# A three-layer model on one core: x's high parts written by ScalarE, low parts taken by VectorE from the turned tiles, and a square that runs one unit behind its product

## The chip, the cores and the metric

The kernel runs on one core of a Trainium2 chip. The metric is the device time of one execution in microseconds (us). Five engines work side by side: TensorE (PE, whose weight loads are shown apart as PEld), VectorE (DVE), ScalarE (ACT), GpSimd (POOL) and SyncE (SP), which here issues the loads of the weights. They meet only at semaphores, and each engine runs its own instructions in the order written.

## What is computed

The input x has 256 tokens of width 1024. Three layers follow: retention, forgetting attention, and a block that has two mixers side by side (dilated window attention and HGRN2) and then a feed-forward part. Cut to what the change touches:

```python
x = x + gate[:, None, :] * y                      # end of the second layer (forgetting attention)
x = _rms_norm(x, final_g)                         # h, the input of the third layer
u = rmsnorm(h, norm1_w[l]); proj = u @ w_in[l]    # "mixers": 7 chunks of 512 columns
ya = dilated_attention_group(qa, ka, va)
yb = hgrn2_group(qb, fb, ib, gb, lb_table[l], hgrn_norm_w[l])
h = h + jnp.concatenate([ya, yb], axis=-1) @ w_out[l]
u2 = rmsnorm(h, norm2_w[l]); gu = u2 @ w_gate_up[l]
h = h + (silu(gate) * up) @ w_down[l]             # "feed-forward"
```

## The kernel before

Every product of float32 matrices is made of three matmuls in a rounded format (fp32r): each operand is split into a high part (its rounded value) and a low part (the rest), and the product is high by high (L354), high by low (L355) and low by high (L356). The operands from x are `ahi` and `alo`, 128x256 for each block of 128 columns, the weights are `whi` and `wlo`.

The weights come as a stream of units of 512 KB, which is two blocks of 128 rows by 512 columns. For each unit SP loads `raw` (8 buffers), ACT writes `whi` (3 buffers; before it writes unit v it waits until PE has finished unit v-3), DVE subtracts to get `wlo`, and PE runs `unit`: 12 matmuls of 512 columns, 6 for each half m of the tokens. On ACT and DVE the call `ring_to(u + 2)` makes the parts of the unit that is two ahead of the one PE is at. All other work of these two engines is written by hand between these calls, so what stands in front of a `ring_to` delays the weights behind it.

Where a layer begins, x has to stand with its columns on the partitions. PE turns four 128x128 blocks of x into one PSUM bank (`x_turn`, 12 of them, n = 0 to 11; n = 4 to 7 belong to the mixers and 8 to 11 to the feed-forward). Before, all twelve then go one way: ACT scales the four blocks from PSUM into a float32 stage in SBUF (`x_act`), DVE copies the stage into `ahi`, rounded, in two instructions, and subtracts to get `alo` in two more (`x_split`). PE may use a block when its `alo` is there (`x_ready`). The four T banks of PSUM go round: `bank()` gives the next one, and PE waits there until the reader of the bank's last tile is done.

The norm in front of the mixers is a double one (of x, and of x times the gain `fg`). So during the first units of the mixers, for each of the four quarters k of x, DVE forms the product `f2` = x * `fg` (signal `f_prod`, L1027 "arena<-x,arena"), and ACT squares and sums first x (`square`, L1765 "acc<-x") and then `f2` (L1765 "acc<-arena", signal `sf1`). `norm_f` on DVE needs all eight sums; ACT takes two roots for it.

Later in the mixers the HGRN2 heads end with `hg_values` (L951, L953, L954), two tiles of PSUM that are made right after the last `values` of the window attention.

Of the kernel before, what the change touches and what calls it, by code (L numbers as in the profile page):

```python
# [6 lines left out]
P = 128  # L7
# [158 lines left out]
def program(nc, x_in, c_in, pos_in, mod_w, mod_b, norm_g, ret_w_in, ret_w_out, fox_w_in, fox_b_f,  # L166
            fox_q_gain, fox_k_gain, fox_w_out, final_g, norm1_w, w_in2, lb_logits, hgrn_nw, w_out2,
            norm2_w, w_gate_up, w_down, final_nw, consts, out):
    with ExitStack() as ctx:
# [154 lines left out]
        def _(e):  # L324
# [7 lines left out]
            def bank(name, sem, n, i=None):  # L332

                if i is None:
                    i = at[0] % 4
                    at[0] += 1
                if ring[i] is not None:
                    on_.wait_ge(*ring[i])
                ring[i] = (sem, n)
                bank_of[name] = i  # L340
                return T[i]
# [50 lines left out]
            def x_turn(src, k0, m):  # L392

                n = turns[0]
                turns[0] += 1
                t = bank(("x", n), sig["x_act"], 2 * SPLIT_ORDER.index(n) + 2)
                transposes(t, [src[:, m, k * P:(k + 1) * P] for k in range(k0, k0 + 4)], "x_turned")

            def x_ready(slot, k0, m, n):
                p = SPLIT_ORDER.index(n)  # L400
                for z in range(2):
                    for k in range(2):
                        ready[slot + k0 + 2 * z + k, m] = (sig["x_split"], 4 * p + 3 + z)


            def turn_x0(k):
# [536 lines left out]
            on_.wait_ge(sig["near"], 16)  # L943
            on_.wait_ge(sig["far"], 1)
            for m in range(2):
                t = bank(("hg_values", m), sig["hg_norm"], 4 + m)
                for h in range(4):
                    vv = vb[:, :, h * P:(h + 1) * P]
                    o = t[:, h * P:(h + 1) * P]
                    if m == 0:  # L950
                        d = e.matmul(o, SH[:, 0, h, :], vv[:, 0, :], start=True, stop=True)  # L951
                    else:
                        e.matmul(o, SH[:, 1, h, :], vv[:, 0, :], start=True, stop=False)  # L953
                        d = e.matmul(o, SH[:, 2, h, :], vv[:, 1, :], start=False, stop=True)  # L954
                d.then_inc(sig["hg_values"], 1)
# [64 lines left out]
        def _(e):  # L1020
# [5 lines left out]
            def tt(o, a, b, op, name):  # L1026
                e.tensor_tensor(o, a, b, op).then_inc(sig[name], 1)  # L1027
# [118 lines left out]
            def x_split(n, slot, k0, m, stage):  # L1146

                p = SPLIT_ORDER.index(n)
                ms = slice(m * P, m * P + P)
                for z in range(2):  # L1150
                    on_.wait_ge(sig["x_act"], 2 * p + z + 1)
                    copy(ahi[:, slot + k0 + 2 * z:slot + k0 + 2 * z + 2, ms], stage[:, (2 * p + z) % 4, :, :], "x_split")
                for z in range(2):
                    b = slot + k0 + 2 * z
                    on_.wait_ge(sig["x_split"], 4 * p + 1 + z)
                    tt(alo[:, b:b + 2, ms], stage[:, (2 * p + z) % 4, :, :], ahi[:, b:b + 2, ms].bitcast(F32), ALU.subtract, "x_split")

            stage1 = acc[:, 2048:3072].rearrange("p (z n s) -> p z n s", z=4, n=2)

# [307 lines left out]
                elif n < 3:  # L1467
                    left_low(10 + 2 * n)
            u_out = {0: u + 1, 1: u + 3}
            stage2 = gate[:, 0, :].rearrange("p (z n s) -> p z n s", z=4, n=2)  # L1470
            ring_to(u + 2)
            ring_to(u + 3)
            add_gated(0, 0, 0, 1, 1, sgf, -1)
            add_gated(1, 0, 1, 1, 1, sgf, -1)
            ring_to(u + 4)
            x_split(4, 16, 0, 0, stage2)
            x_split(5, 16, 0, 1, stage2)
            ring_to(u + 5)
            add_gated(2, 1, 0, 1, 1, sgf, 0)
            add_gated(3, 1, 1, 1, 1, sgf, 1)  # L1480
# [102 lines left out]
            for k in range(4):  # L1583
                ring_to(u + 2)
                u += 1
                if k == 0:
                    x_split(6, 16, 4, 0, stage2)
                    x_split(7, 16, 4, 1, stage2)
                c, m = k // 2, k % 2
                cs_ = slice(512 * c, 512 * c + 512)  # L1590
                on_.wait_ge(sig["mix_in"], 32)
                on_.wait_ge(sig["res1"], 2 * k + 2)
                tt(f2[:, m, cs_], x[:, m, cs_], fg[:, cs_], ALU.mult, "f_prod")
# [94 lines left out]
            add_plain(0, 0, 2)  # L1688
            add_plain(0, 1, 2)
            ring_to(u + 4)  # L1690
            x_split(8, 22, 0, 0, stage2)
            x_split(9, 22, 0, 1, stage2)
            ring_to(u + 5)
            add_plain(1, 0, 2)
            add_plain(1, 1, 2)
# [16 lines left out]
            for c in range(6):  # L1712
                for k in range(4):
                    ring_to(u + 2)
                    u += 1
                    if c == 0 and k == 0:
                        x_split(10, 22, 4, 0, stage2)
                        x_split(11, 22, 4, 1, stage2)
                    if c == 0 and k == 2:
                        r = st[:, 72:74]  # L1720
                        sx = st[:, 64:68].rearrange("p (m c) -> p m c", c=2)
                        on_.wait_ge(sig["sq2"], 4)
                        tt(r, sx[:, :, 0], sx[:, :, 1], ALU.add, "rms2")
                        on_.wait_ge(sig["rms2"], 1)
                        root(r, r, D, "rms2", 0, "rms2_act", 1)
                    if c > 0 and k < 2:
                        left_low(4 * (c - 1) + 2 * k)
                if c < 5:
                    for k in range(4):
                        ring_to(u + 2)  # L1730
# [29 lines left out]
        def _(e):  # L1760
# [31 lines left out]
            def x_act(n, stage, k0, f, scale, shift=None):  # L1792

                p = SPLIT_ORDER.index(n)
                t = T[bank_of["x", n]]
                on_.wait_ge(sig["x_turned"], n + 1)
                for z in range(2):
                    on_.wait_ge(sig["x_split"], 4 * (p - 2) + 3 + z)
                    for i in range(2):
                        k = 2 * z + i  # L1800
                        act(stage[:, (2 * p + z) % 4, i, :], t[:, k * P:(k + 1) * P], f, "x_act" if i else None,
                            scale=scale(k0 + k), bias=shift(k0 + k) if shift else 0.0)

            def sqrt_table():
                on_.wait_ge(sig["filled"], 2)
# [273 lines left out]
                if n in (1, 2):  # L2079
                    left_high(10 + 2 * n)  # L2080
            sqrt_table()
            stage2 = gate[:, 0, :].rearrange("p (z n s) -> p z n s", z=4, n=2)
            ring_to(u + 4)
            on_.wait_ge(sig["rows_read"], 3)
            x_act(4, stage2, 0, ACT.Copy, lambda k: col(n1f, k))
            x_act(5, stage2, 0, ACT.Copy, lambda k: col(n1f, k))
            ring_to(u + 5)
            u += 4

# [18 lines left out]
            def turned_win(n):  # L2108
                m = n % 2
                from_four("wqk", n, (qA, kA)[n // 2][:, :, m * P:(m + 1) * P], ACT.Copy, (0.125, 1.0)[n // 2])  # L2110

            ring_to(u + 2)
            u += 1
            x_act(6, stage2, 4, ACT.Copy, lambda k: col(n1f, k))
            x_act(7, stage2, 4, ACT.Copy, lambda k: col(n1f, k))
            on_.wait_ge(sig["left_turned"], 12)
            for k in range(4):
                if k:
                    ring_to(u + 2)
                    u += 1  # L2120
                c, m = k // 2, k % 2
                cs_ = slice(512 * c, 512 * c + 512)
                square(c, m, 1, 2 * k + 2)
                on_.wait_ge(sig["f_prod"], k + 1)
                on_.wait_ge(sig["sq1"], k + 1)
                act(xn1[:, m, cs_], f2[:, m, cs_], ACT.Square, "sf1", accum=st[:, 68 + 2 * m + c:69 + 2 * m + c])
            for k in range(4):
                ring_to(u + 2)
                u += 1
# [78 lines left out]
                    left_high_scaled(2 * n, 2 * n - 4)  # L2208
            sqrt_table()
            ring_to(u + 4)  # L2210
            x_act(8, stage2, 0, ACT.Copy, lambda k: col(n2_col, k))
            x_act(9, stage2, 0, ACT.Copy, lambda k: col(n2_col, k))
            ring_to(u + 5)
            u += 4

# [4 lines left out]
            for c in range(6):  # L2220
                for k in range(4):
                    ring_to(u + 2)
                    u += 1
                    if c == 0 and k == 0:
                        x_act(10, stage2, 4, ACT.Copy, lambda k: col(n2_col, k))
                        x_act(11, stage2, 4, ACT.Copy, lambda k: col(n2_col, k))
                        on_.wait_ge(sig["left_turned"], 16)
                    if c == 0 and k < 2:
                        for m in range(2):
                            square(k, m, 2, 2 * k + m + 1)  # L2230
                    if c == 0 and k == 2:
                        on_.wait_ge(sig["rms2"], 2)
                        act(st[:, 72:74], st[:, 72:74], ACT.Sqrt, "rms2_act")
                    if c > 0 and k < 2:
                        left_high(4 * (c - 1) + 2 * k)
# [141 lines left out]
```

## Time and profile before

| | |
|---|---|
| median of 3 runs | 735.34 us (732.81 to 736.9) |
| the profiled execution | 736.37 us, span of its core 734.6 us |
| PE busy | 709.7 us, 97% of the span |
| DVE busy | 502.1 us, 68% |
| ACT busy | 380.3 us, 52% |
| mean granted TensorE clock | 0.986 (0.78 in the first 20 us, 1.00 from 60 us to 720 us) |

The span goes from the first to the last instruction; the other 1.8 us of that execution lie around it. The first layer fills the time to about 235 us, the second ends at about 393 us, the mixers begin at about 397 us, the feed-forward at about 541 us. PE is busy nearly all the time, so the stretches where it waits are what matters, and most of the idle time of ACT and DVE costs nothing.

### The profile page before, as it was taken

What the parts mean: (1) busy time and instruction counts of PE and PEld (TensorE: products, weight loads), DVE (VectorE), ACT (ScalarE), POOL (GpSimd) and SP (SyncE); (2) the same over time, 40 slices, a digit from 0 to 9 for tenths busy, and PEclk for the clock granted to TensorE, in tenths of its full rate; (3) what the DMA queues carried; (4) which work ended last, traced back from release to release, by engine and by line L of the source; (5) the groups of instructions that cost most, each with busy time, mean ns of one, the idle gap of its engine ahead of it and who ended that gap; (6) DMA issues with size and microseconds to landing.
All of it is one profiled execution on the core that took longest, in us unless ns stands there. A gap on an engine that the chain in (4) does not pass through costs nothing.

```text
span 734.6 us, 9409 instructions
## 1 busy us (share of the span) xinstructions
PE 709.7 (97%) x3556; PEld 580.8 (79%) x3556; DVE 502.1 (68%) x727; ACT 380.3 (52%) x559; POOL 15.9 (2%) x33
## 2 busy tenths in 40 slices
PE   6999999999999899999999899999999999999996
PEld 5887877777887778878887688887888888888884
DVE  4699887787945868755668599965675555655444
ACT  5347544565534646564555654554565454444343
POOL 6000000000000000000000000000000000000000
PEclk8799999999999999999999999999999999999999
DMA  9999855676964357842454453333456556555611
GB/s 294 370 354 308 298 194 182 201 224 214 309 242 130 123 195 256 266 134 89 138 173 148 141 175 109 122 114 116 139 176 210 189 175 189 182 196 176 198 61 57
DMA packets 74476, 138.96 MB, mean 189 GB/s; under 512 B 5748, under 2 KB 18272, under 8 KB 74432
## 3 DMA queue, kind: packets, MB, share of 16 engines
q1 hardware_dynamic: 72816, 134.82, 56.6%
q10 hardware_dynamic: 736, 1.90, 0.7%
q0 software_dynamic: 880, 1.64, 0.6%
q8 instruction: 28, 0.46, 0.3%
q14 instruction: 16, 0.13, 0.1%
HBM read 137.31 MB, written 1.05 MB: 188 GB/s over the span
## 4 chain that ended last, share of the span: by engine, by line
PE 87%; DVE 7%; ACT 2%; issue 2%; DMA 1%; SPq 0%; DVEq 0%; ACTq 0%
PE G L354 22%; PE G L356 22%; PE G L355 22%; PE T L375 5%; DVE wlo L1027 2%; PE T L741 2%; PE T L854 2%; DVE arena L1027 2%; PE T L731 1%; PE G L465 1%; DMA arena<-in_mod_w_dram 1%; PE G L467 1%; PE G L466 1%; ACT whi L1767 1%; PE T L416 1%
## 5 line engine op out<-in xcount | busy, mean ns | idle before, releaser
L1027 DVE TENSOR_TENSOR wlo<-raw,whi 128x1024 fp32r<-128x1024 f32 x206 | 251.0, 1223 | 133.6 <-ACT whi L1767 133.0
L354 PE MATMUL G<-whi,ahi 128*128 128x512 f32 x776 | 314.4, 405 | 7.4 <-DVE wlo L1027 6.8
L356 PE MATMUL G<-whi,alo 128*128 128x512 f32 x776 | 303.3, 391 | 0.0
L355 PE MATMUL G<-wlo,ahi 128*128 128x512 f32 x776 | 302.3, 390 | 0.0
L1767 ACT ACTIVATE whi<-raw 128x1024 fp32r<-128x1024 f32 x206 | 217.3, 1061 | 131.9 <-PE G L356 117.3
L354 PEld LDWEIGHTS G<-whi,ahi 128*128 128x128 f32 x776 | 145.9, 188 | 41.4 <-DVE wlo L1027 12.1
L356 PEld LDWEIGHTS G<-whi,alo 128*128 128x128 f32 x776 | 145.6, 188 | 32.2
L355 PEld LDWEIGHTS G<-wlo,ahi 128*128 128x128 f32 x776 | 146.1, 188 | 28.5 <-issue 1.2
L1769 ACT ACTIVATE arena<-T,st 128x128 f32<-128x128 f32 (+2 forms) x56 | 21.7, 478 | 30.5 <-DVE st L1400 30.5
L375 PE MATMUL T<-head,arena 128*128 128x128 f32 x244 | 37.2, 277 | 0.0
L375 PEld LDWEIGHTS T<-head,arena 128*128 128x128 f32 x244 | 29.7, 141 | 9.4 <-issue 2.0
L1767 ACT ACTIVATE ahi<-T 128x512 fp32r<-128x512 f32 x25 | 15.0, 599 | 41.5 <-PE T L375 41.5
L1769 ACT ACT_TABLE_LOAD x27 | 34.6, 1283 | 2.8 <-issue 1.8
L1036 DVE SCALAR_TENSOR_TENSOR acc<-raw,cact,acc 128x1024 f32<-128x1024 f32 x24 | 30.8, 1282 | 1.1
L1027 DVE TENSOR_TENSOR alo<-T,ahi 128x512 fp32r<-128x512 f32 x25 | 17.3, 691 | 17.8 <-ACT ahi L1767 17.7
L1027 DVE TENSOR_TENSOR arena<-arena 128x512 f32<-128x512 f32 (+7 forms) x46 | 23.0, 549 | 0.8 <-ACT arena L1769 0.5
L1400 DVE TENSOR_REDUCE st<-T 128x2 f32<-128x512 f32 (+1 forms) x18 | 11.6, 686 | 15.5 <-PE T L731 15.5
L1769 ACT ACTIVATE st<-st 128x1 f32<-128x1 f32 (+3 forms) x21 | 4.3, 206 | 30.0 <-DVE st L1031 18.3
L1036 DVE SCALAR_TENSOR_TENSOR arena<-arena,cact 128x512 f32<-128x512 f32 (+1 forms) x24 | 16.4, 684 | 0.8
L854 PEld LDWEIGHTS T<-arena 128*128 128x128 f32 x128 | 15.4, 191 | 0.9 <-DVE arena L1027 0.4
L1767 ACT ACTIVATE arena<-arena 128x512 f32<-128x512 f32 x14 | 8.3, 640 | 14.4 <-DVE arena L1027 14.4
L854 PE MATMUL T<-arena 128*128 128x128 f32 x128 | 15.7, 276 | 0.0
(219 smaller groups left out, 576.1 us busy)
## 6 DMA issues: line engine op xcount, KB each, us to landing
raw<-in_ret_w_in_dram SPq DMA_DIRECT2D x48, 512.0 KB, 5.4
raw<-in_w_gate_up_dram SPq DMA_DIRECT2D x40, 512.0 KB, 3.8
raw<-in_mod_w_dram SPq DMA_DIRECT2D x32, 512.0 KB, 5.0
raw<-in_fox_w_in_dram SPq DMA_DIRECT2D x32, 512.0 KB, 4.7
raw<-in_w_in_dram SPq DMA_DIRECT2D x28, 512.0 KB, 3.5
raw<-in_w_down_dram SPq DMA_DIRECT2D x22, 512.0 KB, 4.4
arena<-in_mod_w_dram SPq DMA_DIRECT2D x16, 512.0 KB, 8.3
raw<-in_ret_w_out_dram SPq DMA_DIRECT2D x16, 512.0 KB, 5.5
```

Source lines behind the costliest of these rows:

```text
L354: e.matmul(o, ah, wh, start=first and k == 0, stop=False)
L355: e.matmul(o, ah, wl, start=False, stop=False)
L356: done = e.matmul(o, al, wh, start=False, stop=last and k == 1)
L375: d = e.transpose(t[:, n * P:(n + 1) * P], s, idf)
L416: e.matmul(sums_of(SUMMED[g][i], a), mod_tile(g)[:, a, r, i * P:(i + 1) * P], cact[:, r:r + 1], start=r == r0, stop=False)
L741: d = e.matmul(t[:, 65 * a:65 * a + 65], PT[:, g % 2, (a * (m + 1) + j) * P:(a * (m + 1) + j + 1) * P], v[:, j, h, :], start=j == 0, stop= ...
L854: d = e.matmul(t[:, h * P:(h + 1) * P], k[:, h, m * P:(m + 1) * P], q[:, h, m * P:(m + 1) * P], start=True, stop=True)
L1027: e.tensor_tensor(o, a, b, op).then_inc(sig[name], 1)
L1036: e.scalar_tensor_tensor(out=o, in0=a, scalar=s, in1=b, op0=op0, op1=op1).then_inc(sig[name], 1)
L1400: e.tensor_reduce(st[:, 44 + 4 * r:44 + 4 * r + n], t[:, :].rearrange("p (h n) -> p h n", h=n), AX.X, ALU.max, negate=True).then_inc(sig[f ...
L1767: d = e.activation(o, a, f, scale=scale)
L1769: d = e.activation(o, a, f, scale=scale, bias=bias)
```

## The change

For the turned tiles of the mixers and the feed-forward (n = 4 to 11), ACT writes the scaled blocks straight into `ahi`, rounded (`x_high`), and DVE forms `alo` from the PSUM bank, as scale times the turned block minus `ahi` (`x_low`), in one instruction for each block. The bank of such a tile is now free after DVE's last instruction and no longer after ACT's, and DVE waits until ACT has written all four blocks. The square of `f2` for quarter k runs after the weights and the square of x of quarter k+1 (`square_f`). The two tiles of `hg_values` go to the T banks 1 and 2 and no longer take the next two of the round.

```diff
-                t = bank(("x", n), sig["x_act"], 2 * SPLIT_ORDER.index(n) + 2)
+                p = SPLIT_ORDER.index(n)
+                t = bank(("x", n), *((sig["x_act"], 2 * p + 2) if n < 4 else (sig["x_split"], 4 * p + 4)))
...
-                t = bank(("hg_values", m), sig["hg_norm"], 4 + m)
+                t = bank(("hg_values", m), sig["hg_norm"], 4 + m, 1 + m)
...
+            def x_low(n, slot, k0, m, scale):
+
+                p = SPLIT_ORDER.index(n)
+                t, ms = T[bank_of["x", n]], slice(m * P, m * P + P)
+                on_.wait_ge(sig["x_act"], 2 * p + 2)
+                for k in range(4):
+                    b = slot + k0 + k
+                    stt(alo[:, b, ms], t[:, k * P:(k + 1) * P], scale(k0 + k), ahi[:, b, ms].bitcast(F32), ALU.mult, ALU.subtract, "x_split")
...
-            x_split(4, 16, 0, 0, stage2)
-            x_split(5, 16, 0, 1, stage2)
+            x_low(4, 16, 0, 0, lambda k: col(n1f, k))
+            x_low(5, 16, 0, 1, lambda k: col(n1f, k))
...
+            def x_high(n, slot, k0, m, scale):
+
+                p = SPLIT_ORDER.index(n)
+                t, ms = T[bank_of["x", n]], slice(m * P, m * P + P)
+                on_.wait_ge(sig["x_turned"], n + 1)
+                for k in range(4):
+                    act(ahi[:, slot + k0 + k, ms], t[:, k * P:(k + 1) * P], ACT.Copy, "x_act" if k % 2 else None, scale=scale(k0 + k))
...
+            def square_f(k):
+
+                c, m = k // 2, k % 2
+                cs_ = slice(512 * c, 512 * c + 512)
+                on_.wait_ge(sig["f_prod"], k + 1)
+                on_.wait_ge(sig["sq1"], k + 1)
+                act(xn1[:, m, cs_], f2[:, m, cs_], ACT.Square, "sf1", accum=st[:, 68 + 2 * m + c:69 + 2 * m + c])
...
                 square(c, m, 1, 2 * k + 2)
-                on_.wait_ge(sig["f_prod"], k + 1)
-                on_.wait_ge(sig["sq1"], k + 1)
-                act(xn1[:, m, cs_], f2[:, m, cs_], ACT.Square, "sf1", accum=st[:, 68 + 2 * m + c:69 + 2 * m + c])
+                if k:
+                    square_f(k - 1)
+            square_f(3)
```

ACT's instructions behind the second pair of turned tiles of the mixers, before the change (`acc,st<-x` is the square of x, `acc,st<-arena` that of `f2`; after the last row come the two roots of `norm_f`):

```order
L1765 ACTIVATE acc,st<-x 128x512
L1765 ACTIVATE acc,st<-arena 128x512
L1767 ACTIVATE whi<-raw 128x1024
L1765 ACTIVATE acc,st<-x 128x512
L1765 ACTIVATE acc,st<-arena 128x512
L1767 ACTIVATE whi<-raw 128x1024
L1765 ACTIVATE acc,st<-x 128x512
L1765 ACTIVATE acc,st<-arena 128x512
L1767 ACTIVATE whi<-raw 128x1024
L1765 ACTIVATE acc,st<-x 128x512
L1765 ACTIVATE acc,st<-arena 128x512
L1767 ACTIVATE whi<-raw 128x1024
```

And in the changed kernel, at the same place:

```order
L1773 ACTIVATE acc,st<-x 128x512
L1775 ACTIVATE whi<-raw 128x1024
L1773 ACTIVATE acc,st<-x 128x512
L1773 ACTIVATE acc,st<-arena 128x512
L1775 ACTIVATE whi<-raw 128x1024
L1773 ACTIVATE acc,st<-x 128x512
L1773 ACTIVATE acc,st<-arena 128x512
L1775 ACTIVATE whi<-raw 128x1024
L1773 ACTIVATE acc,st<-x 128x512
L1773 ACTIVATE acc,st<-arena 128x512 x2
L1775 ACTIVATE whi<-raw 128x1024
```

The weights' high part now stands between the square of x and the square of the product that belong together, and two squares of `f2` follow each other at the end.

DVE's instructions at the end of the second layer, where the first two turned tiles of the mixers are split, before the change:

```order
L1027 TENSOR_TENSOR x<-x,acc 128x512
L1027 TENSOR_TENSOR wlo<-raw,whi 128x1024
L1039 CAST ahi<-gate 128x2x128 x2
L1027 TENSOR_TENSOR alo<-gate,ahi 128x2x128 x2
L1039 CAST ahi<-gate 128x2x128 x2
L1027 TENSOR_TENSOR alo<-gate,ahi 128x2x128 x2
L1027 TENSOR_TENSOR wlo<-raw,whi 128x1024
L1027 TENSOR_TENSOR acc<-G2,gate 128x512
```

And in the changed kernel:

```order
L1027 TENSOR_TENSOR x<-x,acc 128x512
L1027 TENSOR_TENSOR wlo<-raw,whi 128x1024
L1036 SCALAR_TENSOR_TENSOR alo<-T2,n1f,ahi 128x128 x4
L1036 SCALAR_TENSOR_TENSOR alo<-T3,n1f,ahi 128x128 x4
L1027 TENSOR_TENSOR wlo<-raw,whi 128x1024
L1027 TENSOR_TENSOR acc<-G2,gate 128x512
```

Eight instructions stand where eight stood; they are half as wide as before, have three inputs, and one of these is in PSUM.

PE's instructions at the last `values` of the window attention (L741) and `hg_values` (L951 and on), before the change (T0 to T3 are the four banks):

```order
L354 MATMUL G1<-whi,ahi 128x512
L355 MATMUL G1<-wlo,ahi 128x512
L356 MATMUL G1<-whi,alo 128x512
L741 MATMUL T3<-arena,gate 128x65 x4
L951 MATMUL T3<-arena 128x128 x4
L953 MATMUL T0<-arena 128x128
L954 MATMUL T0<-arena 128x128
```

And in the changed kernel:

```order
L354 MATMUL G1<-whi,ahi 128x512
L355 MATMUL G1<-wlo,ahi 128x512
L356 MATMUL G1<-whi,alo 128x512
L741 MATMUL T3<-arena,gate 128x65 x4
L951 MATMUL T1<-arena 128x128 x4
L953 MATMUL T2<-arena 128x128
L954 MATMUL T2<-arena 128x128
```

The instructions and their order stay; only the banks move, from 3 and 0 to 1 and 2. The instruction in front of them writes to bank 3.

## Rows read from the trace of the kernel before

**Rows 1.** The page, busy time (share of the span) and instructions of each engine.
```profile
PE 709.7 (97%) x3556; PEld 580.8 (79%) x3556; DVE 502.1 (68%) x727; ACT 380.3 (52%) x559; POOL 15.9 (2%) x33
```
**Rows 2.** PE's waits over the span: us in total, times, longest us.
```profile
PE G L354 <- DVE wlo L1027: 6.8, 10, 1.3
...
PE T L951 <- DVE acc L1027: 0.7, 1, 0.7
```
**Rows 3.** Waits of PE's weight loads, 400 to 424 us.
```profile
PEld G L354 <- DVE wlo L1027: 4.7, 5, 1.2
PEld T L375 <- DVE x L1027: 1.3, 2, 0.9
```
**Rows 4.** Stretches: us, busy of PE, PEld, DVE, ACT, POOL, clock, DMA share, GB/s.
```profile
400.00:424.00 24.00, 20.70 (x89) 15.08 (x88) 15.71 (x31) 15.02 (x34) 0.00 (x0) 1.00 0.46 134
430.00:510.00 80.00, 80.00 (x479) 67.70 (x480) 64.14 (x100) 38.66 (x60) 0.00 (x0) 1.00 0.40 125
535.00:555.00 20.00, 20.00 (x97) 16.50 (x96) 14.29 (x29) 13.89 (x32) 0.00 (x0) 1.00 0.59 189
```
**Rows 5.** PE in order of time: start us, us, instruction, [idle before <-releaser].
```profile
402.71 0.40 PE L356 MATMUL G<-whi,alo 128*128 128x512 f32 x1
...
407.50 0.39 PE L356 MATMUL G<-whi,alo 128*128 128x512 f32 x1
408.68 0.50 PE L354 MATMUL G<-whi,ahi 128*128 128x512 f32 x1 [0.79 <-DVE wlo L1027]
...
425.33 0.39 PE L356 MATMUL G<-whi,alo 128*128 128x512 f32 x1
425.56 1.04 PE L375 MATMUL T<-head,arena 128*128 128x128 f32 x8
...
429.31 1.31 PE L375 MATMUL T<-head,arena 128*128 128x128 f32 x8
```
**Rows 6.** ACT in order of time, same place.
```profile
403.46 0.65 ACT L1765 ACTIVATE acc<-x 128x512 f32<-128x512 f32 x1
...
406.25 1.05 ACT L1767 ACTIVATE whi<-raw 128x1024 fp32r<-128x1024 f32 x1
407.21 0.61 ACT L1765 ACTIVATE acc<-x 128x512 f32<-128x512 f32 x1
...
409.26 0.63 ACT L1765 ACTIVATE acc<-arena 128x512 f32<-128x512 f32 x1 [1.35 <-DVE arena L1027]
...
409.89 1.05 ACT L1767 ACTIVATE whi<-raw 128x1024 fp32r<-128x1024 f32 x1
...
419.86 0.47 ACT L1769 ACTIVATE st<-st 128x2 f32<-128x2 f32 x2 [1.64 <-DVE st L1033]
```
**Rows 7.** DVE in order of time, same place.
```profile
404.90 0.69 DVE L1027 TENSOR_TENSOR arena<-x,arena 128x512 f32<-128x512 f32 x1
407.40 1.23 DVE L1027 TENSOR_TENSOR wlo<-raw,whi 128x1024 fp32r<-128x1024 f32 x1 [1.82 <-ACT whi L1767]
408.55 0.68 DVE L1027 TENSOR_TENSOR arena<-x,arena 128x512 f32<-128x512 f32 x1
```
**Rows 8.** ACT and DVE in order of time, turned tiles.
```profile
394.59 2.18 ACT L1767 ACTIVATE gate<-T,n1f 128x128 f32<-128x128 f32 x8 [2.04 <-PE T L375]
...
395.77 0.29 DVE L1039 CAST ahi<-gate 128x256 fp32r<-128x256 f32 x1 [0.22 <-ACT gate L1767]
...
397.05 0.76 DVE L1027 TENSOR_TENSOR alo<-gate,ahi 128x256 fp32r<-128x256 f32 x2
...
397.82 1.23 DVE L1027 TENSOR_TENSOR wlo<-raw,whi 128x1024 fp32r<-128x1024 f32 x1
...
527.38 0.88 DVE L1661 SCALAR_TENSOR_TENSOR alo<-T,cols,ahi 128x256 fp32r<-128x256 f32 x2 [0.99 <-ACT ahi L1767]
```
**Rows 9.** PE's weight loads and PE in order of time, `hg_values`.
```profile
514.34 0.97 PEld L951 LDWEIGHTS T<-arena 128*128 128x128 f32 x8 [0.79 <-issue]
514.37 1.13 PE L951 MATMUL T<-arena 128*128 128x128 f32 x8 [0.68 <-DVE acc L1027]
```

More of the change, by code:

```diff
@@ L400, in x_ready @@
                 p = SPLIT_ORDER.index(n)
-                for z in range(2):
-                    for k in range(2):
-                        ready[slot + k0 + 2 * z + k, m] = (sig["x_split"], 4 * p + 3 + z)
+                for k in range(4):
+                    ready[slot + k0 + k, m] = (sig["x_split"], 4 * p + (3 + k // 2 if n < 4 else 1 + k))
             def turn_x0(k):
@@ L1469, in _ @@
             u_out = {0: u + 1, 1: u + 3}
-            stage2 = gate[:, 0, :].rearrange("p (z n s) -> p z n s", z=4, n=2)
             ring_to(u + 2)
@@ L1586, in _ @@
                 if k == 0:
-                    x_split(6, 16, 4, 0, stage2)
-                    x_split(7, 16, 4, 1, stage2)
+                    x_low(6, 16, 4, 0, lambda k: col(n1f, k))
+                    x_low(7, 16, 4, 1, lambda k: col(n1f, k))
                 c, m = k // 2, k % 2
@@ L1690, in _ @@
             ring_to(u + 4)
-            x_split(8, 22, 0, 0, stage2)
-            x_split(9, 22, 0, 1, stage2)
+            x_low(8, 22, 0, 0, lambda k: col(n2_col, k))
+            x_low(9, 22, 0, 1, lambda k: col(n2_col, k))
             ring_to(u + 5)
@@ L1716, in _ @@
                     if c == 0 and k == 0:
-                        x_split(10, 22, 4, 0, stage2)
-                        x_split(11, 22, 4, 1, stage2)
+                        x_low(10, 22, 4, 0, lambda k: col(n2_col, k))
+                        x_low(11, 22, 4, 1, lambda k: col(n2_col, k))
                     if c == 0 and k == 2:
@@ L1802, in x_act @@
                             scale=scale(k0 + k), bias=shift(k0 + k) if shift else 0.0)
+            def x_high(n, slot, k0, m, scale):
+                p = SPLIT_ORDER.index(n)
+                t, ms = T[bank_of["x", n]], slice(m * P, m * P + P)
+                on_.wait_ge(sig["x_turned"], n + 1)
+                for k in range(4):
+                    act(ahi[:, slot + k0 + k, ms], t[:, k * P:(k + 1) * P], ACT.Copy, "x_act" if k % 2 else None, scale=scale(k0 + k))
             def sqrt_table():
@@ L2081, in _ @@
             sqrt_table()
-            stage2 = gate[:, 0, :].rearrange("p (z n s) -> p z n s", z=4, n=2)
             ring_to(u + 4)
             on_.wait_ge(sig["rows_read"], 3)
-            x_act(4, stage2, 0, ACT.Copy, lambda k: col(n1f, k))
-            x_act(5, stage2, 0, ACT.Copy, lambda k: col(n1f, k))
+            x_high(4, 16, 0, 0, lambda k: col(n1f, k))
+            x_high(5, 16, 0, 1, lambda k: col(n1f, k))
             ring_to(u + 5)
@@ L2110, in turned_win @@
                 from_four("wqk", n, (qA, kA)[n // 2][:, :, m * P:(m + 1) * P], ACT.Copy, (0.125, 1.0)[n // 2])
+            def square_f(k):
[4 more added lines that the diff above has]
+                act(xn1[:, m, cs_], f2[:, m, cs_], ACT.Square, "sf1", accum=st[:, 68 + 2 * m + c:69 + 2 * m + c])
             ring_to(u + 2)
             u += 1
-            x_act(6, stage2, 4, ACT.Copy, lambda k: col(n1f, k))
-            x_act(7, stage2, 4, ACT.Copy, lambda k: col(n1f, k))
+            x_high(6, 16, 4, 0, lambda k: col(n1f, k))
+            x_high(7, 16, 4, 1, lambda k: col(n1f, k))
             on_.wait_ge(sig["left_turned"], 12)
@@ L2210, in _ @@
             ring_to(u + 4)
-            x_act(8, stage2, 0, ACT.Copy, lambda k: col(n2_col, k))
-            x_act(9, stage2, 0, ACT.Copy, lambda k: col(n2_col, k))
+            x_high(8, 22, 0, 0, lambda k: col(n2_col, k))
+            x_high(9, 22, 0, 1, lambda k: col(n2_col, k))
             ring_to(u + 5)
@@ L2224, in _ @@
                     if c == 0 and k == 0:
-                        x_act(10, stage2, 4, ACT.Copy, lambda k: col(n2_col, k))
-                        x_act(11, stage2, 4, ACT.Copy, lambda k: col(n2_col, k))
+                        x_high(10, 22, 4, 0, lambda k: col(n2_col, k))
+                        x_high(11, 22, 4, 1, lambda k: col(n2_col, k))
                         on_.wait_ge(sig["left_turned"], 16)
```

## The prediction

> **What bounds the kernel now.** The page first: PE is busy 97% of the span, DVE 68%, ACT 52% [rows 1]. So a shorter ACT or DVE instruction is worth nothing by itself; the time moves only where PE waits. The list of PE's waits is short, and it is the second view to read: ten waits for the weights' low part, 6.8 us together, and among the single ones 0.7 us of L951 behind an evacuation by DVE [rows 2]. The third view asks where they are. Between 400 and 424 us PE's weight loads waited five times for `wlo`, 4.7 us, and twice for x, 1.3 us [rows 3], and PE was busy 20.70 of 24 us there, against 80.00 of 80 us from 430 to 510 us [rows 4]. That is the place where the square is moved.
>
> How the waits arise is seen in PE's own order [rows 5]. Matmuls start every 0.228 us when nothing holds them: from 402.71 to 407.50 us are 21 steps, 4.79 us. A unit of 12 is then 2.73 us. But the five units behind 407.50 us, up to the matmul of 425.33, take 17.83 us, or 3.57 us each. ACT shows the period, from one `whi` at 406.25 to the next at 409.89 us, 3.64 us [rows 6], and this is a ring over two engines: `whi` to `wlo` 1.15 us (406.25 to 407.40), `wlo` to the product 1.15 us (to 408.55), product to its square 0.71 us (to 409.26), square to the next `whi` 0.63 us (to 409.89) [rows 6, 7]. ACT stands 1.35 us in front of the square of `f2`, waiting for a product that DVE can only make behind the `wlo` that ACT itself has just released. The ring takes 3.64 us where PE needs 2.73, so PE starves.
>
> **The change part by part.**
>
> *The late square.* With the square of `f2` one unit behind, the product it needs has long been made, and nothing goes round. ACT then has for each unit `whi` 0.96 us (406.25 to 407.21) and two squares of some 0.6 us each (0.63 us from 409.26 to 409.89, which includes reading the sum), together 2.2 us; DVE has 1.15 and 0.7 us, together 1.85 us. Both are below PE's 2.73. To see whether the first stall goes too, I walk through it. The square of x is at 403.5 us as now [rows 6]; the `whi` behind it no longer waits for the product and its square, so it starts at some 404.2 instead of 406.25 us, since its buffer has been free since the end of the unit in front of the second turns. Its `wlo` can start at 405.6 us, behind the product that runs at 404.9 us [rows 7], and ends at 406.8 us; PE asks for it at 407.73 us (407.50 plus a step). So the first stall goes with 0.9 us to spare. The next three `whi` then start at 406.4, 408.6 and 412.2 us (the last behind two squares of `f2`, for whose second it waits until 411.6 us), and their `wlo` end at 408.7, 410.9 and 414.5 us, where PE asks at 410.5, 413.2 and 415.9 us. Behind them comes the wait for `norm_f`'s roots, which ACT waits for 1.64 us now [rows 6]: by the same steps the roots run at 415.0 us, the next `whi` at 415.4 us, its `wlo` ends at 417.7 us and PE asks at 418.7 us. This is the tightest place, 1.0 us of slack.
>
> What the five stalls cost: the five units between the matmul of 407.50 and that of 425.33 us [rows 5] are 60 steps, 13.65 us at 0.2275 each; they took 17.83. Term: **-4.2 us**.
>
> *The turn behind it.* DVE comes late to the second turn after this stretch as well: its eight transposes take 1.31 us where the first eight take 1.04 [rows 5]. The norm's two 128x1024 products that stand in front of it on DVE run when the weights' parts ahead of them are done; with those earlier against PE, most of this goes. Of the 0.27 us I take **-0.2 us**. Bounds 0 and -0.3.
>
> *The banks of `hg_values`.* PE waits 0.68 us at L951 because its tile goes to bank 3, which holds the `values` tile made just before it and still to be read by DVE [rows 9]. Bank 1 held the logits and bank 2 the transposed weights of the attention; both were read before that last `values` could start. The wait goes, and with it the whole chain behind (`hg_values` to ACT's square to the norm) is as much earlier. The weight loads show 0.79 us idle. Term: **-0.7 us**. Seven tiles behind it land in other banks, each long free.
>
> *The low parts.* ACT issues 8 blocks of 128x128 for two tiles before and after, in 2.18 us [rows 8]; that the target is `ahi` and rounded, I cost at nothing, because its writes of this format have no longer rows. DVE had 8 instructions and has 8. No 128x128 instruction with scalar and PSUM input is in the trace. The nearest is the 128x256 one: two take 0.88 us [rows 8], so with 0.48 for the last one step is 0.40 us. 128 columns fewer, at about 1.05 ns per column, leave 0.27 us. From above the bound is that same 0.40 us, from below 0.24 us, where ACT's own pace of 0.27 becomes the limit. Now to the chain. DVE can start when ACT has written four blocks, at 395.77 us, where the second CAST starts now; four steps end at 396.84 us, where the second tile has just become ready (ACT ends at 396.77); four more end at 397.91 us. The next `wlo` starts at 397.82 us now [rows 8]. So it is **+0.1 us** late, and at 0.40 us per step it would be +1.2 us late. This is on the path: behind it stand four instructions that add the layer's output to x, and PE waits for them in front of the second turns (the 1.3 us of [rows 3]). That wait stays. Much below nothing it can't go: at 0.24 us a step the second tile still waits for ACT until 396.8 us and ends at 397.8. At the feed-forward the same eight steps stand, but PE is busy 20.00 of 20 us there [rows 4], so +0.1 is covered and of +1.2 us about 1.0 would be felt. For the second pair of tiles at each place PE comes to the blocks a unit later, so there is cover of more than 1 us.
>
> The Trainium skill, "VectorE: DVE Perf Modes", section "The TRN2 errata", speaks against this part: each instruction pays a fixed latency, about twice as long from PSUM as from SBUF, so many small tiles are dear and tiles should have 512 elements or more. An estimate from its figures (58 cycles fixed from SBUF, 120 from PSUM, at 0.96 GHz, the rounding copy at two columns a cycle) is 2.1 us for the old eight and 2.1 us for the new, so that by the page this term is 0 and the sum -5.1 us. The sum below goes by the rows.
>
> *Sum.* -4.2 - 0.2 - 0.7 + 0.1 = -5.0 us, on the profiled execution of 736.37 us (its span of 734.6 and 1.8 around it): 731.4. The median shown, 735.34, is 1.0 us below that execution; the same sum from it gives 730.3, and I take 730.4.
>
> **The rivals.**
>
> *The stall moves instead of going.* For it speaks the 1.0 us of slack at `norm_f`, worked out with steps that I rounded, and the wait of two squares in a row. Against it: later units have 3 us of slack each, so one late `whi` is caught up. One or two stalls of 0.95 us stay: 731.4 to 732.4.
>
> *What is gained is lost later.* PE comes 4 to 5 us earlier to stages with their own chains (the levels of HGRN2, the window attention). For it: DVE is busy 64.14 of 80 us there. Against it: that stage shows no PE wait of its own at all [rows 4], and its chains start from PE's results, so they move along; the weights' transfers are at a share of 0.40 to 0.46. If half is lost: 733.
>
> *The steps of the low parts cost 0.40 us or more.* At 0.40: 1.1 + 1.0 us of the gain are lost, 732.5. This is also the one that **ends on the other side**: two places, each 8 steps, so 16 times the excess over 0.27 us less the cover of about 0.3 us must be over 5.1 us; from 0.61 us per step on the kernel is slower than before. That is nearly what four times the width takes, 0.68 us [rows 7]. It could come if DVE's reads of PSUM held each other up with ACT's beside them, which no row of before shows. At 0.75 us: 737.7. Against it stands the step of 0.40 us at twice the width [rows 8].
>
> *The change doesn't do what it says.* The squares wait for something else, say because DVE makes the product late again behind a late `wlo`. Then only the bank's 0.7 us is left: 734.6.
>
> **How the numbers follow.** 0.5% (3.7 us) is about what a measurement of this kernel can tell from no change, which puts the line at 731.7 us. Chances: all terms as summed 0.68 (its own range 729 to 731.9), stall moves 0.12, half lost later 0.09, dear steps short of slower 0.05, no effect of the square 0.03, slower 0.03. Of the first case nine tenths are below the line, of the second a half, of the dear steps a third: faster 0.69, and slower by 0.5% 0.02, the rest 0.29. The range goes from 728.4 (the stalls' 4.7 us of idle loads instead of 4.2, and runs as low as 2.5 us under their median are shown, of which a median keeps part) to 733.4, which takes in the moved stall and the dear steps.
>
> **What would show it.** In the profile after: no wait of PE for `wlo` between the second turns and the first chunk's end; ACT's squares of `f2` without idle time in front but for the last; units 2.73 us apart there; L951 without a wait; the 128x128 steps of DVE 0.27 us apart; the wait for x in front of the second turns still there, 0.1 us longer. Wrong it would be made by a wait for `wlo` that stays at the unit behind `norm_f`'s roots, or by steps of 0.4 us and more.

## The result and the profile after

The changed kernel takes 729.88 us (median of 7 runs, 729.27 to 731.12) where the kernel before took 736.56 us in the runs beside it. The ratio is 0.9922, with a 95% interval of 0.9904 to 0.9939, so it is 0.6 to 1.0% faster. The forecast was 730.4 us and a gain of 5.0 us. The two medians lie 6.68 us apart, which is more than the traces show below (5.59 us): single runs of the kernel before spread from 732.81 to 737.04 us, so a median of a few still moves by a microsecond (735.34 us from three of them).

The profiled executions differ in how soon they get through the program's first 60 us, a part that no kernel here changes. DVE's first "acc<-raw,cact,acc" starts at 55.03 us in one trace (the kernel with the banks alone, below) and at 58.83 us in that of the change; from there to a table load of ACT at 221.01 and 224.80 us they need 165.98 and 165.97 us. So I read differences of one microsecond not in the spans but in distances within a trace. Two are used: from the first turn of x at the mixers' entry (eight transposes, L375 "T<-head,x") to the first turn of the HGRN2 tiles ("T<-head,arena"), and from the first turn of x to the end of the span, which is known to 0.1 us.

The page's first line, the busy time of each engine, answers to [rows 1]:

```profile
PE 708.7 (97%) x3556; PEld 582.6 (80%) x3556; DVE 501.2 (69%) x727; ACT 379.4 (52%) x559; POOL 15.7 (2%) x33
```

No engine does less work than before: the instruction counts are the same, the busy times of PE, DVE and ACT are within 1.0 us, and the weight loads show 1.8 us more. What has gone is waiting. PE's waits over the whole span, as in [rows 2]:

```profile
PE G L354 <- DVE wlo L1027: 4.3, 6, 1.3
...
PE T L375 <- DVE x L1027: 0.7, 1, 0.7
```

Of ten waits for the low part of the weights six are left (all in the first two layers), and the wait of L951 is no longer there. The one for x at the second turns has stayed, 0.7 us. The stretches (columns as in [rows 4]) say the same: from 415 to 430 us, where PE was busy 13.75 of 15 us before, it is busy throughout. Before, and then after in two rows:

```profile
415.00:430.00 15.00, 13.75 (x63) 10.06 (x61) 12.19 (x20) 9.84 (x15) 0.00 (x0) 1.00 0.57 179
```

```profile
400.00:415.00 15.00, 14.33 (x67) 11.53 (x66) 12.63 (x24) 11.08 (x28) 0.00 (x0) 1.00 0.58 176
415.00:430.00 15.00, 15.00 (x75) 12.56 (x75) 12.31 (x19) 10.94 (x14) 0.00 (x0) 1.00 0.58 175
```

PE in order of time at the mixers' entry, with the four turns of this stage:

```profile
394.24 1.03 PE L375 MATMUL T<-head,x 128*128 128x128 f32 x8
...
402.05 0.66 PE L375 MATMUL T<-head,x 128*128 128x128 f32 x4 [0.67 <-DVE x L1027]
...
421.62 1.03 PE L375 MATMUL T<-head,arena 128*128 128x128 f32 x8
...
425.25 1.03 PE L375 MATMUL T<-head,arena 128*128 128x128 f32 x8
```

And the turns of x before the change:

```profile
393.95 1.03 PE L375 MATMUL T<-head,x 128*128 128x128 f32 x8
...
401.75 0.66 PE L375 MATMUL T<-head,x 128*128 128x128 f32 x4 [0.67 <-DVE x L1027]
```

From the last turn of x to the first of the HGRN2 tiles are 19.57 us (402.05 to 421.62), where they were 23.81 (401.75 to 425.56, the end of it in [rows 5]). The second HGRN2 turn takes 1.03 us, not 1.31.

ACT in order of time, answering to [rows 6]:

```profile
404.38 1.07 ACT L1775 ACTIVATE whi<-raw 128x1024 fp32r<-128x1024 f32 x1
405.32 0.64 ACT L1773 ACTIVATE acc<-x 128x512 f32<-128x512 f32 x1
...
405.94 0.64 ACT L1773 ACTIVATE acc<-arena 128x512 f32<-128x512 f32 x1
...
406.55 1.06 ACT L1775 ACTIVATE whi<-raw 128x1024 fp32r<-128x1024 f32 x1
...
411.75 0.63 ACT L1773 ACTIVATE acc<-arena 128x512 f32<-128x512 f32 x1 [0.74 <-DVE arena L1027]
...
412.38 1.04 ACT L1775 ACTIVATE whi<-raw 128x1024 fp32r<-128x1024 f32 x1
...
415.06 0.47 ACT L1777 ACTIVATE st<-st 128x2 f32<-128x2 f32 x2 [1.63 <-DVE st L1033]
```

The squares of `f2` ("acc<-arena") have no idle time in front but for the last one, and from one `whi` to the next are 2.17 us of work (404.38 to 406.55), less than the 2.73 us of PE's unit.

DVE in order of time, the turned tiles, answering to [rows 8]:

```profile
396.05 2.16 DVE L1036 SCALAR_TENSOR_TENSOR alo<-T,n1f,ahi 128x128 fp32r<-128x128 f32 x8 [0.82 <-ACT ahi L1775]
398.12 1.22 DVE L1027 TENSOR_TENSOR wlo<-raw,whi 128x1024 fp32r<-128x1024 f32 x1
```

Eight instructions take 2.16 us, and one lasts 0.34 us, so they start 0.26 us apart; this distance is called a step. The weights' low part behind them starts 3.88 us after the first turn, and did so 3.87 us after it before (393.95 to the 397.82 of [rows 8]). In that place DVE waits for ACT as well. At the second pair of tiles it has no idle time in front, so there its own work can be compared, before:

```profile
402.75 0.49 DVE L1039 CAST ahi<-gate 128x256 fp32r<-128x256 f32 x2
403.15 0.76 DVE L1027 TENSOR_TENSOR alo<-gate,ahi 128x256 fp32r<-128x256 f32 x2
403.82 0.49 DVE L1039 CAST ahi<-gate 128x256 fp32r<-128x256 f32 x2
404.23 0.76 DVE L1027 TENSOR_TENSOR alo<-gate,ahi 128x256 fp32r<-128x256 f32 x2
```

and after:

```profile
403.05 2.15 DVE L1036 SCALAR_TENSOR_TENSOR alo<-T,n1f,ahi 128x128 fp32r<-128x128 f32 x8
405.12 0.68 DVE L1027 TENSOR_TENSOR arena<-x,arena 128x512 f32<-128x512 f32 x1
```

Up to the product behind them the old eight take 2.15 us (402.75 to the 404.90 of [rows 7]) and the new eight 2.07 (403.05 to 405.12).

PE's weight loads and PE in order of time at L951, answering to [rows 9]:

```profile
509.10 0.97 PEld L951 LDWEIGHTS T<-arena 128*128 128x128 f32 x8
509.16 1.11 PE L951 MATMUL T<-arena 128*128 128x128 f32 x8
```

### The profile page after: what moved, and what is told of

Same layout as the page of the kernel before. It is cut to its first block, busy times and chain, and to the rows that moved or that the text cites. A ratio compares the mean times of both kernels' runs of the same rounds, so it can differ in the third digit from the quotient of the medians.

```text
span 729.3 us, 9397 instructions
## 1 busy us (share of the span) xinstructions
PE 708.7 (97%) x3556; PEld 582.6 (80%) x3556; DVE 501.2 (69%) x727; ACT 379.4 (52%) x559; POOL 15.7 (2%) x33
## 4 chain that ended last, share of the span: by engine, by line
PE 90%; DVE 5%; ACT 2%; issue 1%; DMA 1%; DVEq 0%; ACTq 0%
PE G L354 23%; PE G L356 23%; PE G L355 23%; PE T L375 5%; PE T L741 2%; PE T L854 2%; DVE wlo L1027 1%; PE T L731 1%; DVE arena L1027 1%; PE G L465 1%; PE G L466 1%; PE G L467 1%; PE T L416 1%; DVE acc L1036 1%; PE G L381 1%
## 5 line engine op out<-in xcount | busy, mean ns | idle before, releaser
L375 PE MATMUL T<-head,arena 128*128 128x128 f32 x244 | 36.9, 276 | 0.0
L375 PEld LDWEIGHTS T<-head,arena 128*128 128x128 f32 x244 | 29.8, 141 | 8.9 <-issue 2.0
```

The costliest lines, as they stand in the source:

```text
L375: d = e.transpose(t[:, n * P:(n + 1) * P], s, idf)
```

## The experiments

Distances in us, from one trace of each kernel; both count from the start of the first turn of x, to the first HGRN2 turn and to the end of the span. The ratio is of the times, with its 95% interval.

| kernel | ratio to before | first turn to HGRN2 turn | to the end |
|---|---|---|---|
| before | 1 | 31.61 | 340.65 |
| the change | 0.9922 [0.9904, 0.9939] | 27.38 | 335.06 |
| square alone | 0.994 [0.9924, 0.9957] | 27.35 | 335.95 |
| banks alone | 0.9982 [0.997, 0.9994] | 31.52 | 339.70 |
| turned tiles alone | 0.9999 [0.9985, 1.0012] | 31.47 | 340.51 |
| product ahead | 0.9934 [0.9916, 0.9951] | 28.38 | 336.14 |
| low parts twice, mixers | 0.9978 [0.9967, 0.999] | 30.82 | 338.47 |
| the same, PE filled | 0.9957 [0.994, 0.9974] | 29.45 | 337.20 |
| low parts twice, feed-forward | 0.9944 [0.9926, 0.9962] | 27.37 | 336.55 |
| more squares | 0.9939 [0.9922, 0.9956] | 28.42 | 336.53 |
| turns later | 0.9943 [0.993, 0.9955] | 27.36 | 335.54 |
| turns later, parts ahead | 0.9911 [0.9893, 0.9929] | 26.66 | 334.35 |

**The three parts alone.** Each is the kernel before with one part of the change: `square_f`; the bank of `hg_values`; `x_high` and `x_low`.

```diff
+                if k:
+                    square_f(k - 1)
+            square_f(3)
```

> The kernel before with the late square of f2 alone. Theory (the ring of ACT and DVE is the whole gain of the mixers' first units): the four waits of PE for the weights' low part between 402 and 424 us go, the way from the second turn of x to the first turn of the HGRN2 tiles is 4.2 us shorter and the turn behind it 0.4 us, 4.6 us in all (-0.6%); L951 still waits 0.7 us. Rival (the cheaper split of the turned tiles is what lets the ring keep up): less than half of it, and waits for the low part that stay at 408 us.

```diff
-                t = bank(("hg_values", m), sig["hg_norm"], 4 + m)
+                t = bank(("hg_values", m), sig["hg_norm"], 4 + m, 1 + m)
```

> The kernel before with the banks of hg_values alone. Theory: the wait of 0.7 us at L951 goes and everything behind it is 0.7 to 0.85 us earlier up to the end (-0.1%, too little for the times to tell, so read in the trace). Rival (the gain is given back at ACT, which makes two sigmoid-type outputs of the gate until just then): L951 earlier, the units behind it not.

```diff
-            x_act(4, stage2, 0, ACT.Copy, lambda k: col(n1f, k))
+            x_high(4, 16, 0, 0, lambda k: col(n1f, k))
...
-            x_split(4, 16, 0, 0, stage2)
+            x_low(4, 16, 0, 0, lambda k: col(n1f, k))
```

> The kernel before with the written high parts and the low parts from the turned tiles alone. Theory: no change beyond 0.1 us at the second turns of x and none at the feed-forward, because the eight steps of DVE take as long as the eight before; PE still waits five times for the weights' low part between 402 and 424 us. Rival (this part carries some of the gain, since ACT and DVE lose two hand-overs a tile): 1 us or more faster.

The square alone shortens the way to the HGRN2 turn by 4.26 us and the way to the end by 4.70; the banks shorten the way to the end by 0.95, the tiles by 0.14. Together that is 5.79 us, and the change shows 5.59. PE's waits from 380 to 520 us in the kernel with the square alone:

```profile
PE T L951 <- DVE acc L1027: 0.7, 1, 0.7
PE T L375 <- DVE x L1027: 0.7, 1, 0.7
```

And in the one with the turned tiles alone, the same view:

```profile
PE G L354 <- DVE wlo L1027: 2.5, 4, 0.7
PE T L951 <- DVE acc L1027: 0.7, 1, 0.7
PE T L375 <- DVE x L1027: 0.7, 1, 0.7
```

All three theories held. The tiles do nothing for the ring, and what they gain (0.14 us in the trace, nothing in the times) is no more than the trace can just show. In the kernel with the banks alone L951 is 0.86 us earlier against the first turn and the feed-forward's first turn of x 0.85 us, so nothing is given back at ACT; the rest of the 0.95 us had come before, in a part that this kernel does not change.

**The ring cut at another point.** The changed kernel with the square of `f2` back in its place, and DVE's product in front of the weights' low part:

```diff
             for k in range(4):
-                ring_to(u + 2)
-                u += 1
                 if k == 0:
+                    ring_to(u + 2)
                     x_low(6, 16, 4, 0, lambda k: col(n1f, k))
                     x_low(7, 16, 4, 1, lambda k: col(n1f, k))
...
                 tt(f2[:, m, cs_], x[:, m, cs_], fg[:, cs_], ALU.mult, "f_prod")
+                ring_to(u + 2)
+                u += 1
```

> The changed kernel with the square of f2 back in its old place behind the square of x, and DVE making the product f2 ahead of the weights' low part and no longer behind it. It cuts the same ring at another point. Theory of the ring: only the first stall (0.8 to 1.0 us at 408 us) comes back, because the first square of f2 still stands in front of a high part; the others stay away; 0.9 us slower than the changed kernel, 4.6 us faster than before. Rival (ACT has too much work in these units, and moving a square helped because it spread the load): four stalls of 0.9 us as before, 3.5 to 4 us slower than the changed kernel.

It is 1.00 us longer to the HGRN2 turn than the change (0.9 was said), with one wait left, in PE's order of time:

```profile
399.97 0.66 PE L375 MATMUL T<-head,x 128*128 128x128 f32 x4 [0.67 <-DVE x L1027]
406.80 0.50 PE L354 MATMUL G<-whi,ahi 128*128 128x512 f32 x1 [0.71 <-DVE wlo L1027]
```

ACT does the same squares in the same units as before the change, and 3.2 of the 4.2 us are gone all the same. So it was not too much work on ACT, but the ring.

**What the low parts would have cost.** DVE makes the low parts of one pair of tiles twice, the mixers' first pair or the feed-forward's; the second copy is not read.

```diff
+                    if n in (4, 5):
+                        stt(gate[:, 0, (4 * m + k) * P:(4 * m + k + 1) * P], t[:, k * P:(k + 1) * P], scale(k0 + k), ahi[:, b, ms].bitcast(F32), ALU.mult, ALU.subtract, "again")
                     stt(alo[:, b, ms], t[:, k * P:(k + 1) * P], scale(k0 + k), ahi[:, b, ms].bitcast(F32), ALU.mult, ALU.subtract, "x_split")
```

> The changed kernel in which DVE makes each low part of the first two turned tiles of the mixers twice (the second result into a tile that nobody reads): 8 steps more, 2.1 us of DVE. Theory (this pair stands in front of the four instructions that PE's second turns of x wait for, with no cover): the second turns are 2.1 us later, behind a wait that grows from 0.7 to 2.8 us, and all the rest with them; 732.0 us. Rival (the low parts themselves are needed by PE only a unit later, so they have cover): under 0.5 us.

> The same at the first two turned tiles of the feed-forward. Theory: the same chain, but with some 0.4 us of cover, because the output is added in two instructions there and not in four: 1.7 us later, and a wait of PE for x appears at the second turns. Rival (the place is busy to 20.00 of 20 us, so it has real cover): under 0.5 us. From what both say, the step at which the changed kernel would have been slower than before is worked out.

At the mixers the second turns came 2.07 us later against the first, as said, but the HGRN2 turn 3.44 us later. PE in order of time there:

```profile
401.38 0.66 PE L375 MATMUL T<-head,x 128*128 128x128 f32 x4 [2.04 <-DVE x L1027]
402.71 1.12 PE L375 MATMUL T<-head,x 128*128 128x128 f32 x4 [0.67 <-DVE x L1027]
403.48 0.78 PE L354 MATMUL G<-whi,ahi 128*128 128x512 f32 x1
...
404.48 0.63 PE L356 MATMUL G<-whi,alo 128*128 128x512 f32 x1
404.91 0.63 PE L354 MATMUL G<-whi,ahi 128*128 128x512 f32 x1
...
405.70 0.40 PE L356 MATMUL G<-whi,alo 128*128 128x512 f32 x1
```

Matmuls start 0.43 us apart (404.48 to 404.91), not 0.23. And the stretches (the eighth value is the granted clock) show why:

```profile
400.00:402.00 2.00, 0.61 (x4) 0.42 (x4) 1.93 (x5) 0.00 (x0) 0.00 (x0) 1.00 0.40 80
402.00:404.00 2.00, 1.33 (x6) 1.25 (x6) 2.00 (x4) 1.28 (x5) 0.00 (x0) 0.55 0.47 182
404.00:406.00 2.00, 2.00 (x7) 1.57 (x6) 1.79 (x8) 2.00 (x7) 0.00 (x0) 0.59 0.51 112
406.00:408.00 2.00, 2.00 (x10) 1.63 (x9) 2.00 (x4) 2.00 (x6) 0.00 (x0) 1.00 0.43 163
```

The four transposes at 401.38 us still take 0.66 us, as before the change, the four at 402.71 take 1.12. From about 402 to 405.5 us TensorE has its lower clock, 1.2 GHz, behind a stretch in which it was busy 0.61 of 2 us. At the feed-forward a wait of 1.3 us came, and all was 1.49 us later (1.7 said):

```profile
539.32 1.25 PE L375 MATMUL T<-head,x 128*128 128x128 f32 x8 [1.31 <-DVE x L1027]
```

There the clock stayed at 1.00, though PE was hardly busier in the two microseconds with this wait (0.69 of 2 us) than at the mixers (0.61):

```profile
538.00:540.00 2.00, 0.69 (x6) 0.51 (x6) 2.00 (x4) 0.00 (x0) 0.00 (x0) 1.00 0.12 18
540.00:542.00 2.00, 2.00 (x11) 1.73 (x12) 1.80 (x5) 1.99 (x8) 0.00 (x0) 1.00 0.71 244
```

**Is it the clock?** The same kernel with 16 transposes of the identity on PE in front of the wait, into the bank that is free by then:

```diff
+                for _ in range(filler):
+                    e.transpose(t[:, 0:P], idf, idf)
+                if late is not None:
+                    on_.wait_ge(*late)
...
-                        on_.wait_ge(sig["res1"], 2 * m + 6)
-                        x_turn(x, 4, m)
+                        x_turn(x, 4, m, 16 if m == 0 else 0, (sig["res1"], 2 * m + 6))
```

> The kernel with the doubled low parts at the mixers' first pair showed the second turns 2.07 us later, as said, but the first turn of the HGRN2 tiles 3.44 us later, and a granted clock of 0.55 to 0.59 from 402 to 406 us, behind the stretch in which PE waited 2.0 us. Here PE does 16 transposes of the identity into the free bank in front of that wait, so that it stands idle for less. Theory (the other 1.4 us are the clock, at 1.2 GHz for 3 us): the clock stays at 1.00 and the delay is 2.1 us in all. Rival (they are a second wait on ACT or DVE behind the later turns): 3.4 us again, at full clock.

The delay is 2.07 us at the HGRN2 turn and 2.14 at the end. The stretches, where the filler lies and behind it:

```profile
398.00:400.00 2.00, 1.33 (x11) 0.85 (x8) 1.93 (x4) 0.36 (x2) 0.00 (x0) 1.00 0.62 158
400.00:402.00 2.00, 1.73 (x10) 1.52 (x11) 2.00 (x5) 1.81 (x9) 0.00 (x0) 1.00 0.29 109
402.00:404.00 2.00, 2.00 (x11) 1.63 (x10) 2.00 (x8) 2.00 (x5) 0.00 (x0) 1.00 0.70 207
```

The second turns come at the same distance from the first as without the filler (8.55 us), and yet the HGRN2 turn is 1.4 us earlier (1.3 at the end). The medians, 733.17 and 731.74 us, say the same. So work that computes nothing saved 1.4 us because it kept the clock, and a second wait on ACT or DVE is refuted.

**The slack at `norm_f`.**

```diff
             square_f(3)
+            act(gate[:, 0, :], f2[:, 1, :], ACT.Square, "again")
+            act(acc[:, 2048:3072], f2[:, 0, :], ACT.Square, "again")
```

> The changed kernel with two squares more of 128x1024 on ACT behind the last square of f2 (results that nobody reads), some 1.9 us of ACT. It measures the slack at the roots of norm_f, which the prediction put at 1.0 us (the low part that ends at 417.8 us and is asked for at 418.9). Theory: the first 1.1 us are covered, so the first turn of the HGRN2 tiles is 0.8 us later. Rival (ACT has over 3 us of slack there, as at a unit in the middle of a stage): nothing. Rival (ACT is now the bound): 1.9 us.

The HGRN2 turn came 1.04 us later (0.8 said), and the end 1.47: the weight loads wait twice for `wlo`, and twice for DVE at the second HGRN2 turn, the term that the change had removed.

```profile
PEld G L354 <- DVE wlo L1027: 1.2, 2, 0.8
PEld T L375 <- DVE arena L1031: 0.6, 2, 0.4
```

The two squares are 1.9 us of ACT and cost 1.04 at the first HGRN2 turn, so the slack is real and small, about 0.9 us, and past it a delay costs in two places.

**The wait that stayed.** PE's second turns of x in the middle of the second unit:

```diff
-                unit(u, accs, 16 + 2 * k, k == 0, k == 3)
-                u += 1
-                if k == 0:
+                products(u, 0, accs, 16 + 2 * k, k == 0, k == 3)
+                if k == 1:
                     for m in range(2):
                         on_.wait_ge(sig["res1"], 2 * m + 6)
                         x_turn(x, 4, m)
+                products(u, 1, accs, 16 + 2 * k, k == 0, k == 3)
+                u += 1
```

> The changed kernel with PE's second turns of x (n = 6 and 7) not behind the mixers' first unit but in the middle of the second, behind its half for the first 128 tokens. DVE's last addition to x ends at 402.0 us, and PE is at that place at 402.0 instead of 400.7 us. Theory: the wait of 1.3 us for x is filled by half a unit, and the low parts come just in time for the third unit: 1.0 us faster than the changed kernel, 729.0 us. Rival (the third unit then waits for the low parts of these tiles, whose work now starts half a unit nearer to it): the wait moves there, no gain.

The wait for x went, and nothing was gained (27.36 us to the HGRN2 turn, and 0.48 us longer to the end, because the second HGRN2 turn is late and takes 1.31 us again). The wait had moved, but not to where the rival put it: PE waited at the fourth unit, for the weights' low part.

```profile
407.25 0.50 PE L354 MATMUL G<-whi,ahi 128*128 128x512 f32 x1 [0.47 <-DVE wlo L1028]
```

ACT in order of time shows that the high part it needs stands behind the tiles, while ACT had been idle for 3.40 us in front of them:

```profile
402.12 2.18 ACT L1776 ACTIVATE ahi<-T,n1f 128x128 fp32r<-128x128 f32 x8 [3.40 <-PE T L375]
...
404.75 1.11 ACT L1776 ACTIVATE whi<-raw 128x1024 fp32r<-128x1024 f32 x1
```

**And with that part ahead.** On top of the last one:

```diff
                     x_low(7, 16, 4, 1, lambda k: col(n1f, k))
+                    ring_to(u + 2)
...
-            ring_to(u + 2)
+            ring_to(u + 3)
             u += 1
             x_high(6, 16, 4, 0, lambda k: col(n1f, k))
...
                 square(c, m, 1, 2 * k + 2)
-                if k:
-                    square_f(k - 1)
+                if k == 3:
+                    ring_to(u + 2)
+                if k > 1:
+                    square_f(k - 2)
+            square_f(2)
             square_f(3)
```

> With the later turns alone the wait for x went, but 0.9 us came back at the fourth unit's low part (ACT makes the high part of that unit behind the turned tiles, and they are now later) and 0.4 us at the second turn of the HGRN2 tiles. Here ACT makes the fourth unit's high part in front of the turned tiles, where it stands idle for 3.4 us; DVE makes its low part in front of the first product f2; the squares of f2 run two units behind; and one more high part stands in front of the last three squares. Theory: no wait of PE for x or the weights' low part is left from 398 us to the first chunk's end; 1.0 to 1.1 us faster than the changed kernel, 729 us or a little under. Rival (DVE has no room: low parts, product and weights' low part are 4 us in a row there): a wait of 0.5 us or more at the third or fourth unit, no gain beyond 0.5 us.

It takes 728.67 us, ratio 0.9911; in the traces it is 0.72 us ahead of the change at the HGRN2 turn and 0.71 at the end. By the times the two can't be told apart, since their intervals overlap. What is left of the 1.0 us said lies in two short waits of the weight loads, 0.29 us each, behind which PE's matmuls are some 0.3 us late in all:

```profile
402.36 0.19 PEld L354 LDWEIGHTS G<-whi,ahi 128*128 128x128 f32 x1 [0.29 <-issue]
405.23 0.19 PEld L354 LDWEIGHTS G<-whi,ahi 128*128 128x128 f32 x1 [0.29 <-DVE wlo L1028]
```

## Why the prediction was right, step by step

*The late square, -4.2 us.* 4.24 us in the change's trace and 4.26 with the square alone. All five stalls of the weight loads between 400 and 424 us went. The walk through the first units held to some 0.3 us: said were starts of `whi` at 404.2, 406.4, 408.6, 412.2 and 415.4 us, measured 404.38, 406.55, 408.73, 412.38 and 415.43 in a trace that is 0.3 us later at the first turn. That the ring and not ACT's load was the cause is shown by the kernel with the product ahead.

*The turn behind it, -0.2 us.* This term was too small, it was 0.4 us: the second HGRN2 turn starts 3.63 us after the first (3.75 before) and is 0.28 us shorter. I had counted only the length that the rows showed, taken off a quarter of it, and left out the late start.

*The banks, -0.7 us.* 0.84 us: 5.51 us gained at L951 against 4.67 at the `values` in front of it, counted from the last turn of x. The 0.79 us by which the weight loads stood idle was the better reading of this wait than the 0.68 us of the matmul.

*The low parts, +0.1 us.* 0.0 at this place. The step is 0.26 us, where 0.27 was taken and 0.40 the bound. The Trainium skill's fixed costs ("VectorE: DVE Perf Modes", section "The TRN2 errata") had given an estimate of 2.1 us for the old eight and 2.1 us for the new; the trace agrees, with 2.15 and 2.07 us at the second pair. The wait for x at the second turns stayed at 0.7 us, as said.

*The sum* is then 5.5 us in the trace against 5.0 forecast, nearly all of the difference in two small terms, the turn and the banks, that were put too low. That the time of 730.4 us comes as near as 0.5 us to the measured 729.88 is in part luck: it was reckoned from a median of 735.34 us, and the kernel before took 736.56 beside the change and 734.94 beside the first experiments. The gain in the traces is the fairer test of the sum.

*The rivals.* No stall moved, though it would have from 0.9 us more on ACT. Nothing was lost later: from L951 to the turns of the feed-forward both kernels need the same 23.3 us. For the rival of dear steps, the one that ends on the other side, the chain was right and the price too low: I had the cost of dearer steps rise evenly, and 0.61 us a step as the point from which the kernel is slower than before. With twice the steps at the mixers' pair (0.52 us per block) the delay was 3.41 us, of which 1.3 us are the clock, and at the feed-forward's 1.49 us. The two add up to 4.9 of the 5.6 us gained; the 0.7 us left, over 16 steps, put the point near 0.56 us a step. By the ratios the two cost 0.56% and 0.22%, which is the whole 0.78% gained, so it may lie as low as 0.52 us. Both are estimates, as the two at once were not run.

## What to carry to other kernels

Where a busy engine waits with an even period that is longer than its own work, write down the period's parts from two helper engines' rows: if they add up to the period, the helpers wait for each other in a ring, and moving one link by one unit removes it, without any work getting less. Then walk the new order through with the measured durations and look for the place with the least slack; a wait that is filled elsewhere comes back where an engine's in-order queue has the next needed thing behind it. And when a wait of TensorE gets longer, look at the granted clock behind it: here one of 2.04 us cost 1.4 us more than itself, and one of 1.31 us did not.

## What the runs showed of the hardware

TensorE's clock fell from 2.4 to 1.2 GHz in a stretch in which PE waited 2.04 and then 0.67 us with four transposes between. It stayed low for about 3.5 us, with matmuls that start 0.43 us apart, and cost 1.4 us beside the wait. It stayed at 1.00 at a wait of 0.67 us and one of 1.67 us (the change, at 402 and 239 us), at one of 1.31 us (low parts twice, feed-forward), and where 16 transposes filled the wait of 2.04 us down to 0.28. What separates the one case from the others, no run here shows.

ACT takes the same 2.18 us for eight scaled blocks of 128x128 from PSUM, whether they go to a float32 tile or, rounded, to `ahi`. Eight scaled subtractions of DVE of 128x128 with one input in PSUM take 2.07 us; four rounding copies and four subtractions of twice the width from SBUF take 2.15 (both at the second pair of tiles).
